# Gated delta rule inside a two-block fp32 transformer: the queries' norm statistic as two products of rounded squares, placed after the gate's first unit

## What is computed

```python
qkv = silu(causal_dwconv(concat([dq, dk_, dv_]), dn_conv_w))      # 8 heads, 128 features each
cq, ck, cv = split(qkv)
cq = l2norm(cq)                      # x * rsqrt(sum(x*x) + EPS), per token and head
ck = l2norm(ck)
# per head and chunk of 128 tokens:
A    = strict_lower((k*beta) @ k.T * L)          # L: decay between two tokens
u, w = solve(I + A, [v*beta, k*beta*exp(G)])     # triangular solve
attn = lower(q @ k.T * L)
# state S over the chunks: v_new = u - w S;  o = q_dec S + attn v_new;  S = S*d + k_dec^T v_new
```

## Time and profile before

| | before |
|---|---|
| median of 3 runs | 2244.84 us (2244.69 to 2245.06) |
| span of the profiled execution, first to last instruction | 2243.1 us |
| granted TensorE clock in the span | 0.999 |
| TensorE busy | 2224.7 us (99%) |
| VectorE, ScalarE, GpSimd busy | 952.6, 873.2, 1016.2 us |

### The profile page before, as it was taken

How to read it: one execution, slowest core, us unless ns; L and a number is a source line. 1 busy time by engine, 2 the same in 40 slices (tenths; PEclk the granted TensorE clock), 3 DMA queues, 4 the chain that set the end, 5 groups by cost and what they waited for, 6 DMA issues and landing times.

```text
span 2243.1 us, 25574 instructions
## 1 busy us (share of the span) xinstructions
PE 2224.7 (99%) x10856; PEld 1836.8 (82%) x10856; DVE 952.6 (42%) x1171; ACT 873.2 (39%) x1080; POOL 1016.2 (45%) x431
## 2 busy tenths in 40 slices
PE   9999999999999999999999999999999999999998
PEld 7888878888888887888888877888878888888887
DVE  6251225342143403253414634168587224666603
ACT  4354334232322443332334536255664534332222
POOL 5427334444444472355443632434333454465643
PEclk9999999999999999999999999999999999999999
DMA  6215223323332341233233431344241233333322
GB/s 236 98 60 167 75 66 96 102 94 94 101 96 94 114 151 47 94 95 102 94 108 99 127 85 47 99 129 100 62 117 48 85 132 96 101 94 95 102 94 76
DMA packets 161090, 222.86 MB, mean 99 GB/s; under 512 B 24256, under 2 KB 87744, under 8 KB 160720
## 3 DMA queue, kind: packets, MB, share of 16 engines
q1 hardware_dynamic: 159136, 216.08, 31.0%
q10 hardware_dynamic: 1840, 5.15, 0.7%
HBM read 214.34 MB, written 6.85 MB: 99 GB/s over the span
## 4 chain that ended last, share of the span: by engine, by line
PE 95%; DVE 3%; ACT 1%; issue 0%; DMA 0%; POOL 0%; SPq 0%; DVEq 0%; ACTq 0%
PE ps L1224 82%; PE ps L1448 2%; PE ps L1461 1%; PE ps L1486 1%; PE ps L1445 1%; PE ps L1574 1%; PE ps L1310 1%; PE ps L1604 1%; PE ps L1563 0%; DVE ACC L1865 0%; PE ps L1619 0%; PE ps L1582 0%; PE ps L1631 0%; PE ps L1612 0%; PE ps L1474 0%
## 5 line engine op out<-in xcount | busy, mean ns | idle before, releaser
L602 POOL TENSOR_TENSOR w_lo<-w_raw,w_hi 128x1024 fp32r<-128x1024 f32 x378 | 972.8, 2583 | 1187.5 <-ACT w_hi L689 1172.1
L689 ACT ACTIVATE w_hi<-w_raw 128x1024 fp32r<-128x1024 f32 x378 | 396.2, 1056 | 885.2 <-DMA w_raw<-w_in 124.6
L1224 PE MATMUL ps<-XH,w_hi 128*128 128x512 f32 x1760 | 688.5, 391 | 0.0
L1224 PE MATMUL ps<-XH,w_lo 128*128 128x512 f32 x1760 | 685.0, 389 | 0.0
L1224 PE MATMUL ps<-XL,w_hi 128*128 128x512 f32 x1760 | 684.8, 389 | 0.0
L1224 PE MATMUL ps<-HID,w_hi 128*128 128x512 f32 x1728 | 533.1, 390 | 0.1
L1224 PEld LDWEIGHTS ps<-XH,w_hi 128*128 128x128 f32 x1760 | 330.4, 188 | 69.5 <-issue 1.2
L1224 PEld LDWEIGHTS ps<-XH,w_lo 128*128 128x128 f32 x1760 | 330.3, 188 | 69.3
L1224 PEld LDWEIGHTS ps<-XL,w_hi 128*128 128x128 f32 x1760 | 330.4, 188 | 68.8 <-issue 1.2
L1224 PEld LDWEIGHTS ps<-HID,w_hi 128*128 128x128 f32 x1728 | 324.2, 188 | 68.4 <-issue 1.0
L1224 PE MATMUL ps<-HID,w_lo 128*128 128x512 f32 x864 | 336.1, 389 | 0.0
(11 more groups left out here) (398 smaller groups left out, 2228.5 us busy)
## 6 DMA issues: line engine op xcount, KB each, us to landing
w_raw<-w_in SPq DMA_DIRECT2D x72, 512.0 KB, 3.8
w_raw<-ffn_w_up SPq DMA_DIRECT2D x128, 256.0 KB, 2.9
w_raw<-w_up SPq DMA_DIRECT2D x88, 256.0 KB, 3.0
w_raw<-xa_wkv SPq DMA_DIRECT2D x32, 512.0 KB, 3.7
w_raw<-ffn_w_down SPq DMA_DIRECT2D x32, 512.0 KB, 3.8
w_raw<-w_in_c SPq DMA_DIRECT2D x24, 512.0 KB, 3.8
w_raw<-w_down SPq DMA_DIRECT2D x22, 512.0 KB, 3.7
w_raw<-xa_wq SPq DMA_DIRECT2D x16, 512.0 KB, 3.8
```

The lines of the kernel that those rows point to most:

```text
L602: nc.gpsimd.tensor_tensor(w_lo[:, s, :, :], w_raw[:, s, :, :], w_hi[:, s, :, :].bitcast(F32), ALU.subtract).then_inc(lo_done, 1)
L689: nc.scalar.activation(w_hi[:, s, :, :], w_raw[:, s, :, :], ACT.Copy).then_inc(hi_done, 1)
L1224: mm = nc.tensor.matmul(ps[:, bank + m, :], a, b, start=start and j == 0 and n == 0, stop=stop and j == 1 and n == 2)
```

## The change

Three things are done for each q. The sums of the queries' squares are no longer four plain products but eight of the rounded kind: ScalarE writes `SQH`, the rounded squares, GpSimd the rest `SQL` (four instructions, in place over `SQq`, which moves to another address), and each bank gets two products. They are moved behind gate unit 0, and the keys' transposes take their place ahead of it. On ScalarE `KD` is moved ahead of `VB`, and a split ahead of `inverse_norm`. GpSimd's new step `query_squares` stands ahead of `lo` of unit `u0 + 14`, and `expand` waits for the statistic as well, since `MM` and `MTP` lie over `SQq`.

```diff
--- before.py
+++ after.py
@@ -249,7 +249,7 @@
         T1 = at("T1", 56, [P, 4, NCH * HALF])
         GX = H[:, 4:8, :]
         SQk, LNk = at("SQk", 56, [P, 4, T]), at("LNk", 56, [P, 4, T])
-        SQq, LNq = at("SQq", 56, [P, 4, T]), at("LNq", 56, [P, 4, T])
+        SQq, LNq = at("SQq", 48, [P, 4, T]), at("LNq", 56, [P, 4, T])
         SQo, LNo = at("SQo", 48, [P, 4, T]), at("LNo", 56, [P, 4, T])
         SQL, SQH = at("SQL", 48, [P, 4, T], F32R), at("SQH", 56, [P, 4, T], F32R)
         EGA = at("EGA", 88, [P, 4, T])
@@ -643,6 +643,7 @@
                 nc.gpsimd.tensor_copy(VC[64:P, tile, :], V[64:P, src, :]).then_inc(pool_done, 1)
             pool.wait_ge(pool_done, 8)
             def expand(q):
+                pool.wait_ge(l2_st, 2 * q + 2)
                 for i, (pk, m) in enumerate(((PKM, MM), (PKT, MTP))):
                     pool.wait_ge(pk_loaded, 32 * (q + 1))
                     for hh in range(4):
@@ -651,6 +652,12 @@
                             pk[:, 4 * hh:4 * hh + 4, :].unsqueeze(2).broadcast_to([P, NCH, HALF // FIRST, FIRST]),
                             BD[:, :, :].unsqueeze(1).broadcast_to([P, NCH, HALF // FIRST, FIRST]), ALU.mult).then_inc(mx_pool, 1)
 
+            def query_squares(q):
+                pool.wait_ge(l2_sq, 3 * q + 3)
+                for c in range(4):
+                    nc.gpsimd.tensor_tensor(SQL[:, c, :], SQq[:, c, :], SQH[:, c, :].bitcast(F32),
+                                            ALU.subtract).then_inc(w0_and_stat_lo, 1)
+
             def out_squares(q):
                 pool.wait_ge(do_sq, 3 * q + 3)
                 for c in range(4):
@@ -658,7 +665,9 @@
                                             ALU.subtract).then_inc(w0_and_stat_lo, 1)
 
             for u in range(early + 4, n_units):
-                if u == first["dkqv1"] + 5:
+                if u in (first["dkqv0"] + 10 + LEAD, first["dkqv1"] + 10 + LEAD):
+                    query_squares(int(u > first["dkqv1"]))
+                elif u == first["dkqv1"] + 5:
                     out_squares(0)
                 elif u == first["dz"] + 5:
                     out_squares(1)
@@ -1053,6 +1062,10 @@
                 def square(i, x, sq):
                     act.wait_ge(dq_act, 7 * q + i + 1)
                     nc.scalar.activation(sq[:, :, :], x[:, :, :], ACT.Square).then_inc(l2_sq, 1)
+
+                def square_hi():
+                    act.wait_ge(l2_sq, 3 * q + 2)
+                    nc.scalar.activation(SQH[:, :, :], SQq[:, :, :], ACT.Copy).then_inc(l2_sq, 1)
 
                 def inverse_norm(i, ln):
                     act.wait_ge(l2_st, 2 * q + i + 1)
@@ -1095,16 +1108,17 @@
                 silu(1, QN)
                 act.wait_ge(l2_n, 4 * q + 2)
                 square(1, QN, SQq)
+                square_hi()
                 split_to(u0 + 12 + LEAD)
+                act.wait_ge(dp_be, 4 * q + 4)
+                act.wait_ge(dp_eg, 4 * q + 4)
+                scaled_rows(KD, 3, 16 * q + 4, A)
                 act.wait_ge(dq_dve, 47 * q + 35)
                 for c in range(4):
                     nc.scalar.activation(VB[:, c, :], GX[:, c, :], ACT.Copy,
                                          scale=pcol("dn_conv", 3 * 3 * DN_H + 2 * DN_H + 4 * q + c)).then_inc(dq_act, 1)
+                split_to(u0 + 13 + LEAD)
                 inverse_norm(1, LNq)
-                split_to(u0 + 13 + LEAD)
-                act.wait_ge(dp_be, 4 * q + 4)
-                act.wait_ge(dp_eg, 4 * q + 4)
-                scaled_rows(KD, 3, 16 * q + 4, A)
                 act.wait_ge(fs_dve, FS * q + FS - 1)
                 nc.scalar.activation(FST[:, :, :], FSM[:, :, :].rearrange("p a b -> p b a"), ACT.Copy).then_inc(fs_dve, 1)
                 split_to(u0 + 15 + LEAD)
@@ -1254,7 +1268,7 @@
                     pe.wait_ge(acc_done, 7 * (n + 1))
                     bank = STAT_BANK_IN if name == "in0" else STAT_BANK
                     if name in STAT_SPLIT:
-                        pe.wait_ge(w0_and_stat_lo, 1 + STAT_SPLIT.index(name) + 1 + (8 if name == "up2" else 0))
+                        pe.wait_ge(w0_and_stat_lo, 1 + STAT_SPLIT.index(name) + 1 + (16 if name == "up2" else 0))
                         nc.tensor.matmul(ps[:, bank, :], ONES_R[:, :], ACC_HI[:, :], start=True, stop=False)
                         mm = nc.tensor.matmul(ps[:, bank, :], ONES_R[:, :], ACC_LO[:, :], start=False, stop=True)
                     else:
@@ -1598,10 +1612,19 @@
                 def in_chunks(n):
                     return slice(n * P, (n + 1) * P)
 
-                def squares(i, sq):
-                    pe.wait_ge(l2_sq, 2 * q + i + 1)
+                def key_squares():
+                    pe.wait_ge(l2_sq, 3 * q + 1)
                     for c in range(4):
-                        mm = nc.tensor.matmul(ps[:, A + c, :], ones, sq[:, c, :], start=True, stop=True)
+                        mm = nc.tensor.matmul(ps[:, A + c, :], ones, SQk[:, c, :], start=True, stop=True)
+                    mm.then_inc(l2_st, 1)
+
+                def query_squares():
+                    pe.wait_ge(rows_act, 17 * q + 4)
+                    pe.wait_ge(l2_sq, 3 * q + 3)
+                    for c in range(4):
+                        nc.tensor.matmul(ps[:, A + c, :], ONES_R[:, :], SQH[:, c, :], start=True, stop=False)
+                        pe.wait_ge(w0_and_stat_lo, OUT_LO + 8 * q + c + 1)
+                        mm = nc.tensor.matmul(ps[:, A + c, :], ONES_R[:, :], SQL[:, c, :], start=False, stop=True)
                     mm.then_inc(l2_st, 1)
 
                 def keys_by_keys():
@@ -1620,12 +1643,11 @@
                         mm.then_inc(kv_pe, 1)
 
                 def keys_transposed():
-                    pe.wait_ge(l2_ln, 2 * q + 2)
+                    pe.wait_ge(at_dve, 8 * q + 4)
                     transposed(KN, A)
 
                 def keys_by_queries():
                     pe.wait_ge(l2_n, 4 * q + 4)
-                    pe.wait_ge(rows_act, 17 * q + 4)
                     for hh in range(4):
                         for n in range(NCH):
                             mm = nc.tensor.matmul(ps[:, A + hh, in_chunks(n)], KN[:, hh, in_chunks(n)], QN[:, hh, in_chunks(n)],
@@ -1679,11 +1701,10 @@
                     pe.wait_ge(do_ln, 1)
                 group(u0 + 4, 4, B, XH, XL)
                 pe.wait_ge(dq_dve, 47 * q + 1)
-                squares(0, SQk)
+                key_squares()
                 pe.wait_ge(dq_dve, 47 * q + 18)
                 group(u0 + 8, 4, B, XH, XL, after=keys_by_keys)
-                pe.wait_ge(at_dve, 8 * q + 4)
-                squares(1, SQq)
+                keys_transposed()
                 pe.wait_ge(dq_dve, 47 * q + 35)
                 nl = 28 * q
 
@@ -1692,7 +1713,7 @@
                     pe.wait_ge(mx_pool, 8 * q + hh + 1)
                     level_inner(hh)
 
-                group(first[f"gated{q}"], 4, B, XH, XL, first_after=keys_transposed, after=keys_by_queries, last=first_level)
+                group(first[f"gated{q}"], 4, B, XH, XL, first_after=query_squares, after=keys_by_queries, last=first_level)
                 for hh in range(4):
                     pe.wait_ge(mx_pool, 8 * q + 4 + hh + 1)
                     pe.wait_ge(lv_dve, nl + hh + 1)
@@ -1749,7 +1770,7 @@
                     pe.wait_ge(do_sq, 3 * q + 3)
                     for c in range(4):
                         nc.tensor.matmul(ps[:, 4 + c, :], ONES_R[:, :], SQH[:, c, :], start=True, stop=False)
-                        pe.wait_ge(w0_and_stat_lo, OUT_LO + 4 * q + c + 1)
+                        pe.wait_ge(w0_and_stat_lo, OUT_LO + 8 * q + 4 + c + 1)
                         mm = nc.tensor.matmul(ps[:, 4 + c, :], ONES_R[:, :], SQL[:, c, :], start=False, stop=True)
                     mm.then_inc(do_st, 1)
                 return emit
```

## The result

| | before | changed |
|---|---|---|
| median | 2244.99 us (20 runs) | 2248.54 us (20 runs, 2248.03 to 2250.08) |
| ratio, 95% interval | | 1.0016 (1.001 to 1.0022) |
| span of the profiled execution | 2243.1 us | 2246.4 us |
| granted TensorE clock | 0.999 | 0.999 |

The forecast was 2248.5 us. All 20 runs of the changed kernel lie above all 20 of the kernel before (up to 2245.64 us). The changed kernel's own page first: TensorE is busy 1.5 us less than in the kernel before, and takes longer.

A forecast was written before the change was run, and what follows sets the result against it. TensorE was taken to bound the kernel, with VectorE leading behind the gate. VectorE's 9.2 us of lateness less 5.5 of room gave +3.7 us: 2248.5 us against the runs' median 2244.84, range 2244.8 to 2250.8.

The forecast's parts named there:

- TensorE's saving: Queries' statistic on TensorE: eight rounded products (1.87 us) replace four plain ones (3.44 us), -1.57 us a pass.
- room: VectorE's waits for TensorE at `ATT` and fourth `lower_block`, 5.0 us over both passes, plus 0.5, absorb lateness before the level step.
- The cover of `evacuate(2)`: Ahead of gate unit 0: the transposes hide VectorE's `evacuate(2)` less than the old statistic did, so TensorE waits 0.6 us.
- ScalarE: ScalarE's queue: logarithm's table load 5.2 us later, at 1545.1, so VectorE could normalise from 1550.7, 3.6 us later.
- GpSimd beside the inverses: `block_inverses` on VectorE waits for three GpSimd `lo` steps, 7.1 us less overlap, ending near 1554.2, 7.0 us later.
- the upper bound: Short inverse instructions on VectorE wait out every GpSimd instruction in full: +3.7 us in all; the other bound gives +1.7.
- The sum: Up to the level step: VectorE late by 4.8 + 4.4 = 9.2 us, less 5.5 of room, +3.7 us.
- Rival 1: At the inverses: short instructions aren't held up, the exponential is late instead, 3.6 us a pass; +1.7 us, chance 0.2.
- Rival 2: At the level step: VectorE isn't late at all, so TensorE's saving stands, -3.1 to -1.8 us; chance 0.07.
- Rival 3: At `expand`: its steps hit more taps or memory is slower, up to 1.6 us more a pass, +6.9; chance 0.2.

The follow-up runs named there:

- run 6: Changed kernel with two splits moved ahead of the queries' squares and their two GpSimd `lo` steps ahead of `SQL`: 2243.77 us, ratio 0.9994 to the kernel before.
- run 7: Changed kernel with two splits and their `lo` steps ahead of the squares' steps, third split back behind the exponentials: 2243.83 us, ratio 0.9995 to the kernel before.
- run 2: Changed kernel's order, but the statistic still four plain products, without `SQH` and `SQL`: 2246.83 us, ratio 1.0008 to the kernel before.
- Run 3: Kernel before plus three extra GpSimd `tensor_tensor` steps reading SBUF beside the inverses in each pass: 2252.5 us, ratio 1.0035.
- run 4: Kernel before plus three extra GpSimd memsets, which read nothing from SBUF, beside the inverses in each pass: 2245.1 us, ratio 1.0.
- Run 1: Changed kernel with GpSimd's three `lo` steps behind `SQL` held back until VectorE's inverses are done: 2249.46 us, ratio 1.002 to the kernel before.
- run 5: Rounded statistic in the old place ahead of gate unit 0, ScalarE's order as before but for `SQH`: 2253.33 us, ratio 1.0036 to the kernel before.

## Why the prediction was right

- **TensorE's saving.** Expected -1.57 us a pass. The eight products take from 1542.80 to about 1544.7, as those from 1616.15 to 1618.02 did. Runs 6 and 7 show that it reaches the time once VectorE's lateness fits its room; in run 6 VectorE waits for TensorE again in `delta(1)`.
- **The cover of `evacuate(2)`.** Expected 0.6 us a pass, measured 0.64 of wait, and 0.26 more in the first product behind it (run 2). This term was sized at two thirds. In the changed kernel it is hidden by VectorE's lateness.
- **ScalarE.** The table load was expected at 1545.1 and stands at 1545.03. That this is not what decides was worked out ahead, and run 2 shows it: as late, and no wait for it.
- **GpSimd beside the inverses.** The one price of which no row of before showed an instance. I took the upper bound, three `lo` steps in full, and the inverses' end at 1554.2: it stands at 1554.0. Of the 6.8 us that they end later, 6.4 are the three `lo` steps, where I had 7.0, and 0.4 the `tensor_scalar` ahead of them, which I had left out. Run 3 makes the same thing in the kernel before, run 4 that it is the reads. The Trainium skill ("SBUF — State Buffer", section "Who interferes with whom") says that a VectorE instruction with two SBUF inputs contends with a GpSimd instruction that reads SBUF, and not with one that only writes it; by that rule, the trace agrees: 2461 ns and 228 ns at most.
- **The sum.** VectorE later by 4.8 and 4.4 us at `ATT`, less 5.5 of room, +3.7 us. `ATT` begins at 1560.93, where VectorE was free at 1557.43 - 0.91 = 1556.5: 4.4 us later, a term 0.4 too large; in `delta(1)` it is 4.1, where I had 4.4. The level step came 1.94 and 1.25 us later, +3.2, where I had 2.1 and 1.6. The spans of the profiled executions differ by 3.3 us and the medians by 3.55, so the agreement of 2248.5 with 2248.54 is closer than the terms are: that last half a microsecond is luck. The waits of VectorE at `ATT` and the fourth `lower_block` are gone, as expected.
- **Rival 1** (+1.7 us, short instructions not held up) is out by the three rows of 2.33 us. **Rival 2** (a saving at once) is out by the waits. Rival 1's sum was wrong as well. It charged the exponential's 3.6 us in full and forgot the 2.2 us that the normalisation gains once no `lo` meets it, which I had taken off in my own sum: 1.4 us of lateness, less than the room. Run 2 does have +1.9 us, but from TensorE's wait, while the late exponential cost nothing. **Rival 3** (the expansion worse) did not come: the taps beside it took 4.59 us in `delta(0)` and 4.16 in `delta(1)`, where they took 4.32 and, by the same timeline, 4.55. TensorE waited 1.2 us for the expansion in `delta(0)`, under VectorE's lateness.
- **Left open.** The run-to-run range of the changed kernel is 2 us, that of before 1; why is not settled. Run 1 was 0.9 us slower than the changed kernel, by medians of different sets, and this was read from one profile each.

## What to carry to other kernels

When work is given to GpSimd, ask what VectorE does meanwhile, and count both ways: a GpSimd instruction that reads SBUF adds about its whole length to VectorE work with two SBUF operands, if it falls on it (here 7.1 us of `lo` steps made the chain of inverses 6.4 us longer), and moving it later only changes which instruction pays. It was free where VectorE idled (run 6), and where VectorE read one of two operands from PSUM: an instruction of `ATT` beside the expansion took 0.67 us in the changed kernel, as one of `AT` did with GpSimd idle. An instruction with a single SBUF operand isn't safe by that alone, as the `tensor_scalar` shows. And a saving on the bounding engine counts only up to the room that the engine it waits for next has: here some 2.7 us a pass, to be read from that engine's waits before anything else is worked out.

## What was not expected of the hardware

A chain of short dependent VectorE instructions isn't spared: each waiting `tensor_tensor` of 0.19 us took 2.33 us, and in the changed kernel exactly one gets through between two GpSimd instructions. Three 128x1024 memsets on GpSimd (1.0 us each) beside the same chain left it at 228 ns at most. And TensorE, which did a single product between a wait of 0.94 us and one of 0.80 us, was then granted half its clock (run 5: 0.98 of it in 1534 to 1537, 0.50 in 1537 to 1542), where the single wait of 0.6 us in the changed kernel left it at 1.00.
